# Routed experts in rounds of one, two or four, ranked by token count on the chip

## What is computed

```python
def moe_ffn(h, router_w, router_bias, w_gate, w_up, w_down, ws_gate, ws_up, ws_down):
    scores = sigmoid(xt @ router_w)                      # 256 tokens x 64 experts
    sel = scores + router_bias                           # 4 of 8 groups, then the top 8 experts
    wts = scores of the 8 chosen, / their sum * 2.5
    y = for each expert e:  (silu(x_e @ w_gate[e]) * (x_e @ w_up[e])) @ w_down[e],  times wts
    return sum over a token's 8 experts + the shared expert of the same form
```

## Time and profile before

| | us |
|---|---|
| median of 3 executions | 3715.33 |
| lowest, highest | 3712.76, 3722.76 |
| the profiled execution: its time, its span | 3722.76, 3722.7 |
| first layer's expert loop in it, first transposes to the first operation behind it | 342.95 to 937.40 |
| second layer's | 1251.00 to 1899.90 |
| busy: PE, PEld, DVE, ACT, POOL | 3370.9, 2469.4, 1214.7, 650.1, 215.4 |
| mean granted clock of PE | 0.956 |

### The profile page before, as it was taken

One profiled execution on the slowest core, in us unless ns is written; L12 is line 12 of the kernel. 1 busy time (PEld: TensorE's weight loads), 2 busy tenths in 40 slices (PEclk: granted clock), 3 DMA queues, 4 the chain that ended last, 5 costly groups with the idle time before them and its releaser, 6 DMA issues.

```text
span 3722.7 us, 68873 instructions
## 1 busy us (share of the span) xinstructions
PE 3370.9 (91%) x29944; PEld 2469.4 (66%) x29944; DVE 1214.7 (33%) x2371; ACT 650.1 (17%) x1258; POOL 215.4 (6%) x186
## 2 busy tenths in 40 slices
PE   7998899999888889999979999999998889887899
PEld 5776466666667556656657664448877777786788
DVE  1344132233334323323345452010324454444200
ACT  0111011111110111111123231000023313332100
POOL 0000000000000000000000000000004410341000
PEclk9998999999899899999989999999999999998999
DMA  7655398899474469969912351224431013100342
GB/s 275 221 216 224 152 386 331 349 402 385 161 273 154 181 245 372 402 274 382 392 67 81 137 191 68 79 78 149 147 141 48 4 34 125 37 4 3 128 155 102
DMA packets 116171, 703.07 MB, mean 189 GB/s; under 512 B 11296, under 2 KB 11472, under 8 KB 49760
## 3 DMA queue, kind: packets, MB, share of 16 engines
q1 hardware_dynamic: 112224, 685.47, 47.5%
q0 software_dynamic: 3584, 12.25, 1.0%
HBM read 696.62 MB, written 1.05 MB: 187 GB/s over the span
## 4 chain that ended last, share of the span: by engine, by line
PE 41%; DVE 5%; ACT 2%; issue 1%; POOL 1%; DVEq 0%; ACTq 0%; POOLq 0%; PEldq 0%
PE ps L1518 9%; PE ps L1505 9%; PE ps L2148 7%; PE ps L204 4%; PE ps L1855 4%; DVE arena L137 2%; ACT arena L120 1%; PE ps L544 1%; PE ps L571 1%; PE ps L342 1%; PE ps L2530 1%; PE ps L2160 1%; PE ps L2153 1%; DVE arena L141 1%; PE ps L559 1%
## 5 line engine op out<-in xcount | busy, mean ns | idle before, releaser
L204 PE MATMUL ps<-arena 128*128 128x256 f32 (+2 forms) x2432 | 637.8, 425 | 45.6 <-issue 17.1
L204 PEld LDWEIGHTS ps<-arena 128*128 128x128 f32 (+1 forms) x2432 | 475.8, 197 | 201.6 <-issue 124.6
L120 ACT ACTIVATE arena<-ps 128x512 f32<-128x512 f32 (+1 forms) x526 | 265.2, 504 | 1632.6 <-PE ps L204 384.9
L1098 PE MATMUL ps<-arena 128*64 128x256 f32 x4096 | 484.9, 387 | 33.1 <-issue 32.9
L1098 PEld LDWEIGHTS ps<-arena 128*64 128x64 f32 x4096 | 320.3, 140 | 198.1 <-issue 91.6
L2148 PE MATMUL ps<-arena 64*64 64x64 f32 x10496 | 310.4, 226 | 53.6 <-issue 19.5
L1505 PE MATMUL ps<-arena 128*128 128x512 f32 (+1 forms) x1024 | 334.1, 489 | 10.3 <-DVE arena L146 10.3
L2148 PEld LDWEIGHTS ps<-arena 64*64 64x64 f32 x10496 | 296.9, 141 | 67.7 <-issue 34.5
L1518 PE MATMUL ps<-arena 128*128 128x256 f32 x1536 | 332.0, 379 | 0.0
L1518 PEld LDWEIGHTS ps<-arena 128*128 128x128 f32 x1536 | 291.8, 190 | 40.1 <-issue 0.5
L137 DVE TENSOR_TENSOR arena<-arena,ps 128x512 f32<-128x512 f32 (+1 forms) x276 | 163.1, 591 | 461.1 <-PE ps L2148 237.9
(11 more groups left out here) (190 smaller groups left out, 2557.8 us busy)
## 6 DMA issues: line engine op xcount, KB each, us to landing
arena<-in_w_gate SPq DMA_DIRECT2D x128, 1024.0 KB, 8.5
arena<-in_w_up SPq DMA_DIRECT2D x128, 1024.0 KB, 11.7
arena<-in_w_down SPq DMA_DIRECT2D x128, 1024.0 KB, 8.9
arena<-in_mlp SPq DMA_DIRECT2D x80, 1024.0 KB, 4.7
arena<-in_w_ada SPq DMA_DIRECT2D x48, 1024.0 KB, 7.2
arena<-in_ada SPq DMA_DIRECT2D x48, 1024.0 KB, 4.8
arena<-in_w_in SPq DMA_DIRECT2D x30, 1024.0 KB, 5.6
arena<-in_w_rkv SPq DMA_DIRECT2D x20, 1024.0 KB, 4.8
```

The costliest lines, as they stand in the source:

```text
L120: self.e.activation(out, in_, func, bias=bias, scale=scale, **more).then_inc(*self.done(key))
L204: ins = pe.matmul(out, a, b, start=start and i == 0, stop=stop and i == len(pairs) - 1)
L1098: ins = pe.matmul(psum.of["gu", l, new][64 * ab:64 * ab + 64, i_ * 256:i_ * 256 + 256], xe[:, k, new % 2 * 128 + 64 * ab:new % 2 * 128 + 6 ...
```

## The change

The experts are no longer taken by number. Their counts of tokens are made on the chip, the experts are ranked by them, and the rank says in which *place* an expert is computed. The 64 places lie in 26 rounds (13 pairs) of one, two or four places, with 128, 64 or 32 slots each:

| pair | 0 | 1 | 2 | 3 | 4 | 5 | 6 | 7 to 11 | 12 |
|---|---|---|---|---|---|---|---|---|---|
| places in each of its two rounds | 2 | 1 | 4 | 2 | 4 | 1 | 4 | 2 | 4 |

Places 0 to 3 belong to experts 16 to 19 whatever their counts, so that their weights can be loaded before the ranking is known. The four fullest of the others go to the rounds of one, the next 24 to the other rounds of two, the last 32 to the rounds of four. Counts in the reference's inputs, from its own routing:

| layer | experts over 64, with their old rounds | in rounds of one | in rounds of two, most | in rounds of four, most |
|---|---|---|---|---|
| first | 109, 99, 73 tokens; rounds 2, 3, 14 | 109, 99, 73, 56 | 55 | 31 |
| second | 67, 75, 71, 73 tokens; rounds 1, 2, 19, 31 | 75, 73, 71, 67 | 63 | 30 |

What comes with it:

- **Before the loop, PE and DVE.** New matmuls count the tokens and turn the mask and the gates to expert-major (L1070 to L1079 of the changed kernel), five DVE operations rank the experts and make a permutation matrix, five more matmuls move mask, gates and numbers into rank order (L1113 to L1116), DVE copies them out, and only then come the matmuls of the places and all that hangs on them. The shared down projection is split in two halves around them.
- **SP.** From round 2 on every expert load first reads the expert's number from SBUF into a register, and its address in HBM is computed from it. Before the first of them SP waits for the numbers.
- **In the loop.** The same matmuls for each expert, on 128, 64 or 32 columns; all else once a round, so 26 times and not 32. The overflow test stands as it was, with 128, 64 or 32 as the limit.

```diff
+PLAN = (2, 1, 4, 2, 4, 1, 4, 2, 2, 2, 2, 2, 4)
+FIRST = (16, 17, 18, 19)
+WIDTH = [n for n in PLAN for _ in range(2)]
...
+        def expert_rows(sp, name, l, e):
+
+            if e < len(FIRST) or at.counting:
+                return D[name][l, FIRST[e % len(FIRST)]]
+            o = 192 + l * 64 + e
+            chosen = sp.value_load(flags[0:1, o:o + 1], min_val=0, max_val=63)
+            src = D[name][l, bass.ds(chosen, 1)]
+            return src.rearrange("o p j d -> (o p) j d" if name == "w_down" else "o p n -> (o p) n")
...
                 if new is not None:
+                    if new == 2:
+                        sp.wait_ge(*at["ids", l])
                     for name in ("w_gate", "w_up", "w_down"):
-                        for e in (2 * new, 2 * new + 1):
+                        for e in places_of(new):
+                            src = expert_rows(sp, name, l, e)
...
+                load(sp, (name, l, e), ("up", l, new), src, also=[("over", "pe", l, new)])
...
+            down(shared[2], True, False, (0,))
+            b, old = psum.hold(3, ("sorted", l), ("ids", l))
+            freed(pe, old)
+            reach(pe, *at["moved", l])
...
+            down(shared[2], True, False, (1,)).then_inc(*made(("shared", l)))
...
                 def hidden(i_, what):
-                    for ab in range(2):
-                        reach(pe, *at[what, l, 2 * new + ab])
+                    w = 128 // WIDTH[new]
+                    for e in places_of(new):
+                        reach(pe, *at[what, l, e])
                     for k in range(8):
-                        for ab in range(2):
+                        for ab in range(WIDTH[new]):
...
+            do.stt(E.at[:, 0:1], b[0:64, 64:65], 64.0, E.key_col[0:64, :], ALU.mult, ALU.add)
+            do.stt(E.keys, b[0:64, 0:64], 64.0, E.key_row[0:64, :], ALU.mult, ALU.add)
+            do.ts(E.keys, E.keys, E.at[:, 0:1], None, ALU.is_gt, None)
+            do.red(E.at[:, 1:2], E.keys, ALU.add)
+            do.ts(E.moved, E.rank_at[0:64, :], E.at[:, 1:2], None, ALU.is_equal, None, ("moved", l))
+            b = psum.of["sorted", l]
+            dve.wait_ge(*at["sorted", l])
+            do.cp(mk, b[:, 0:128], ("mask in order", l))
+            do.cp(flags[0:1, 192 + l * 64:256 + l * 64], b[0:1, 256:320])
```

More of the change, by code:

```diff
@@ L21, with places_of @@
 NPUMP = (2, 6)
+PLAN = (2, 1, 4, 2, 4, 1, 4, 2, 2, 2, 2, 2, 4)
+FIRST = (16, 17, 18, 19)
+WIDTH = [n for n in PLAN for _ in range(2)]
+NQ, NR = len(PLAN), len(WIDTH)
+BASE = [sum(WIDTH[:r]) for r in range(NR + 1)]
+assert BASE[-1] == 64 and 2 * PLAN[0] == len(FIRST)
+def places_of(r):
+    return range(BASE[r], BASE[r + 1])
 ARENA = 35144
@@ L1033, in moe_pe @@
                     .then_inc(*made(("shared gu", l, j)))
-            b, old = psum.hold(2, ("places", l), ("counts", l))
+            b, old = psum.hold(2, ("loads", l), ("moved", l))
             freed(pe, old)
-            reach(pe, *at["tri"])
-            reach(pe, *at["shared h", l, 1])
-            pe.matmul(b[:, 0:64], tri[:, 0:128], E.mk[:, 0:64], start=True, stop=True)
-            pe.matmul(b[:, 64:128], tri[:, 0:128], E.mk[:, 64:128], start=True, stop=False)
-            pe.matmul(b[:, 64:128], ones[:, :], E.mk[:, 0:64], start=False, stop=True)
-            pe.matmul(b[:, 128:192], ones[:, :], E.mk[:, 0:64], start=True, stop=False)
-            pe.matmul(b[:, 128:192], ones[:, :], E.mk[:, 64:128], start=False, stop=True).then_inc(*made(("places", l)))
+            reach(pe, *at["weighed", l])
+            for t in range(2):
+                pe.matmul(b[0:64, 0:64], ones[:, 0:64], E.mk[:, t * 64:t * 64 + 64], start=t == 0, stop=t == 1)
+            for t in range(2):
+                ins = pe.matmul(b[0:64, 64:65], E.mk[:, t * 64:t * 64 + 64], ones[:, 0:1], start=t == 0, stop=t == 1)
+            ins.then_inc(*made(("loads", l)))
+            b, old = psum.hold(3, ("by expert", l), ("by expert out", l))
+            freed(pe, old)
+            for i, (v, n) in enumerate(((E.mk, 64), (E.Gt, 65))):
+                for t in range(2):
+                    o = i * 256 + t * 128
+                    ins = pe.transpose(b[0:64, o:o + 128], v[:, t * n:t * n + 64], ident[:, :])
+            ins.then_inc(*made(("by expert", l)))
             for i in range(4):
@@ L1045, in moe_pe, with down @@
                 freed(pe, old)
-            def down(wd, first, last):
+            def down(wd, first, last, tiles_=(0, 1)):
                 wv = wd.rearrange("p (j d) -> p j d", j=2)
-                for t in range(2):
+                for t in tiles_:
                     for nh in range(2):
@@ L1068, in moe_pe @@
             reach(pe, *at["ws_down", l])
-            down(shared[2], True, False).then_inc(*made(("shared", l)))
+            reach(pe, *at["shared h", l, 1])
+            down(shared[2], True, False, (0,))
+            b, old = psum.hold(3, ("sorted", l), ("ids", l))
+            freed(pe, old)
+            reach(pe, *at["moved", l])
+            for t in range(2):
+                pe.matmul(b[:, t * 64:t * 64 + 64], E.mkT[:, t * 128:t * 128 + 128], E.moved, start=True, stop=True)
+            for t in range(2):
+                pe.matmul(b[:, 128 + t * 64:192 + t * 64], E.GtT[:, t * 128:t * 128 + 128], E.moved, start=True, stop=True)
+            pe.matmul(b[0:32, 256:320], E.index[0:64, :], E.moved, start=True, stop=True) \
+                .then_inc(*made(("sorted", l)))
+            down(shared[2], True, False, (1,)).then_inc(*made(("shared", l)))
+            b, old = psum.hold(2, ("places", l), ("counts", l))
+            freed(pe, old)
+            reach(pe, *at["tri"])
+            reach(pe, *at["mask in order", l])
+            pe.matmul(b[:, 0:64], tri[:, 0:128], E.mk[:, 0:64], start=True, stop=True)
+            pe.matmul(b[:, 64:128], tri[:, 0:128], E.mk[:, 64:128], start=True, stop=False)
+            pe.matmul(b[:, 64:128], ones[:, :], E.mk[:, 0:64], start=False, stop=True)
+            pe.matmul(b[:, 128:192], ones[:, :], E.mk[:, 0:64], start=True, stop=False)
+            pe.matmul(b[:, 128:192], ones[:, :], E.mk[:, 64:128], start=False, stop=True).then_inc(*made(("places", l)))
             for k in range(0, 8, 2):
@@ L1113, in moe_pe @@
                     reach(pe, *at["htt", l, p])
-                    for ab in range(2):
-                        reach(pe, *at["w_down", l, 2 * p + ab])
+                    w = 128 // WIDTH[p]
+                    for e in places_of(p):
+                        reach(pe, *at["w_down", l, e])
                     for nh in range(2):
```

105 lines of the change are left out of this document (64 added, 41 removed).

## The result

| | median, us | lowest to highest | ratio to before, 95% |
|---|---|---|---|
| before | 3719.05 | 3712.76 to 3724.66 | |
| the change | 3604.27 | 3600.54 to 3608.04 | 0.969 (0.9676 to 0.9703) |
| predicted | 3533 | 3490 to 3640 | |

The change is faster by 3.1%, 115 us where 182 were forecast. The profiled execution took 3605.11 us, its span is 3603.3.

The account below looks back on a forecast made before the run. PE and weight DMA nearly tie, with seven overflow blocks adding 203 us; without them transfer binds. Loops fall from 1243 to 1040 us (-203), ranking adds 21: -182, so 3533 us against the median, range 3490 to 3640.

Parts of the forecast that it names:

- A: Expert loops: overflow blocks vanish and the weights' transfer becomes the bound; own range 3490 to 3575 us, chance 0.55.
- B: Rounds of four: PE stays at the lower clock after its waits, 64 us in all, 3597 us; chance 0.2.
- C: Expert loads: tiles come slower through the register or from scattered experts; 3625 us at a tenth slower; chance 0.12.
- rival E: Expert loops: an overflow block still runs, one costs 29 us, giving 3565 us; chance 0.06.
- SP's 1.3 us for a tile: SP's queue: register load, DMA and address instruction cost 1.3 us a tile, hidden below the transfer's 2.51.
- D: SP's queue: each load costs more than 3.0 us, making the kernel slower; at 3.5 us 3850 us; chance 0.07.
- the forecast 10.6 each: Ahead of each layer's loop: counting, ranking and added DVE work cost 10.6 us a layer, 21 in all.
- the release 2.4 us later: Rounds of four: SP's next load was taken to start 2.4 us after the up projection ends.
- the term of 12 us for the eight rounds of four: Each layer's rounds of four: idle DMA time from slow projections after short waits, 12 us, bounds 0 and 44.
- the 30.5 us: Rounds of four: from one slot release to the next plus restart, 30.5 us against 32.3 when DMA engines run dry.
- the tile's price: Weights' transfer in the loops: one tile of 1.049 MB costs 2.51 us, at most 2.60.
- half of 18: Second layer's loop: three of six pump tiles fall in rounds of two; half their 18 us taken, 8 us counted.

Follow-up runs that it names:

- e3: The change with all 16 pairs as rounds of two, still ranked and loaded through registers (overflow blocks return): 3701.9 us.
- e2: The change without any overflow test in the rounds of four, their overflow handling left out on all three engines: 3560.8 us.
- g1: The change with the overflow block of a round of four handling only its last expert, the test kept: 3572.4 us.
- f1: The change with SP's wait for the w_gate and w_up slots moved from TensorE's overflow counter to ScalarE's: 3573.4 us.
- g2: f2 plus, in rounds of four but the last two, SyncE making the overflow test and freeing gate slots after the gate projection: 3553.4 us.
- f2: The change with DVE's rounding of x put ahead of its waits for the sorted and counted masks: 3591.3 us.
- e4: The change with 28 more transposes per expert in the never-run overflow block of the rounds of two: 3632.1 us.
- e1: The change with each round of four's overflow test split into two, each jumping over two experts' block: 3608.1 us.

## Why the prediction was off

The measured 3604 lies in the stated range, but 29 us above the own range of the forecast mechanism (A, to 3575). The room that it fell into was there for rivals B and C, which did not come true; that part is luck.

**Right in direction and in most of the mechanism.** No block ran: rival E falls. The loops became bound by the weights' transfer. PE waits 136.6 us in 15 stretches for in_w_gate, and in rounds of two the DMA engines are always busy. SP's 1.3 us for a tile was measured at 1.2 and is hidden (D falls), and tiles land 2.5 us apart through registers as without (C falls; e3). Rounds of four pack as forecast. 8.9 and 8.2 us ahead of the loops stand for the forecast 10.6 each, and PE's first gather comes 10.1 us later (344.92 for 334.78). That "the DMA engines are idle there" was read wrong: before, they are busy 0.72 of the time from 334 to 343 us. They fill the ring, in the change from 331 to 341, and are done ahead of the loop, so the added time counts all the same. The trace after has 415 GB/s over 123 us of rounds of two. The 358 GB/s of the Trainium skill, "DMA: Bandwidth & Descriptors", section "Where 436 GB/s comes from", by which about 3688 us would have come out, is not what holds here.

**The step that failed** is the sentence "the release 2.4 us later", in the term of 12 us for the eight rounds of four. It was measured on a round of two. In a round of four with its full block the release came 8.2 us after the up projection, since PE's branch stood for 6.0 us, over four experts' program text. With that, release to release is not the 30.5 us that "just fit" under 32.3 but about 36. The rows of a round's transposes between 410 and 560 us show it (first and last start, which are those of rounds 5 and 10): the change's, then e2's, g1's and f1's.

```profile
L1148 PEld LDWEIGHTS ps<-ident,arena x12: 140/142/230, 423.0 to 559.3; 128*128 128x128 f32 x12
```

```profile
L1148 PEld LDWEIGHTS ps<-ident,arena x12: 140/142/143, 421.9 to 543.5; 128*128 128x128 f32 x12
```

```profile
L1154 PEld LDWEIGHTS ps<-ident,arena x12: 140/142/143, 420.0 to 544.9; 128*128 128x128 f32 x12
```

```profile
L1148 PEld LDWEIGHTS ps<-ident,arena x12: 140/184/231, 424.4 to 555.7; 128*128 128x128 f32 x12
```

136.3 us, 121.6 without the test, 124.9 with the short block, 131.3 with the release by ScalarE. The step of a pair's second round of four alone, from its transposes to the next ones, takes 35.2 to 36.4 us in the change (six such steps), 28.5 to 31.3 in e2 and 29.4 to 31.4 in g1. The forecast 30.5 fits the short branch.

**The sizes of the rest.** Of the loops' 62 us over forecast (1102.4 for 1040), 33 go with the long branch (g1), 12 more with the test itself (e2), which I had counted at nothing in a round with slack. That was wrong, because the slack is PE's while the release is on the transfer's path. 17 are left: 1.5 from where the loop is taken to end, and the others, by an estimate that no run tested, the tile's price. Two windows of e2, one with rounds of four and one with rounds of two alone, have full DMA engines at 402 and at 414 GB/s:

```profile
490.00:580.00 90.00, 64.39 (x523) 43.67 (x522) 20.58 (x41) 11.55 (x20) 0.00 (x0) 0.89 0.98 402
...
660.00:803.00 143.00, 137.81 (x990) 95.58 (x989) 45.36 (x88) 27.11 (x47) 0.00 (x0) 1.00 1.02 414
```

A tile at 402 GB/s costs 2.61 us, the 2.6 that I had named as the most and left for 2.51; over half the tiles of a layer that is 9 us, 18 in both layers, by this estimate a little more than the 15.5 that are left.

The other terms can be set beside the DMA engines' idle time, added up from the packets over the stretches in which less than 0.6 of the engines' time is used. At the start it is 10 us a layer for the 11 forecast. At the rounds of one it is 17 and 24 us for 24. At and behind the rounds of four it is 29 and 30 us in the change and 11 and 13 in e2, for the 12 forecast: with the release at 2.4 us or less this term would have been right. Two slips of the sum change little: half of 18 is 9, not 8, for the pumps, and 3597 + 48 is 3645, not 3640, for the range's end.

**Rival B** gives 3597 and so lies nearest to 3604, but not by its mechanism. Its sign, idle DMA engines inside the rounds of four, did come, but the branch gives the same sign. After PE's wait of 12.49 us ahead of round 5's gate projection the clock is at its lower level (1.2 GHz, granted share 0.50), and that projection takes 5.9 us and not 3.66:

```profile
430.00:440.00 10.00, 4.03 (x40) 2.51 (x44) 0.00 (x0) 0.00 (x0) 0.00 (x0) 0.50 1.01 424
440.00:450.00 10.00, 8.64 (x127) 4.35 (x118) 1.50 (x2) 1.38 (x2) 0.00 (x0) 0.97 0.79 308
```

But by the up projection it is back at the full one (0.97, 2.4 GHz; 3.66 us), where B had all three projections at 7.1. What the 2.2 us at the gate projection cost was not tried by itself.

Of the 203 us forecast for the loops 142 were thus measured. Three quarters of the missing 61 (45) went into a wait that the change made itself, at the test of the rounds of four, where the text that a round skips is twice that of before; the rest is put down to the tile's price by an estimate. The fastest version, g2, gets 51 us back (3553.4), some 13 of them by f2's order of DVE's work, still with all overflow handling; with these inputs its overflow paths, as those of the change, are never taken, so only the path without overflow was timed.

## What to carry to other kernels

A branch over code that is never run is not free. On PE its price rose with the program text skipped, though not for every branch (e4), and it falls on everything that the same queue releases afterwards. Give buffers back ahead of such a test, or by an engine whose branch is short (ScalarE's took 45 ns here), and look at the queue's own branch rows, which no busy time shows. Where a transfer is the bound, a slack of 15 us on the computing engine hides its work but not a delay in what frees the next buffer: cost each such release by its own row, in the shape that the change will have.

## What was not expected of the hardware

PE's branch takes mostly 0.2 to 0.5 us (at most 2.4) over the text of one or two experts and 1.4 to 6.8 us over that of four. The long ones end 2.3 to 2.6 us after a 16 KB packet of program text starts, and this packet starts up to 4.4 us after the branch does. Splitting one jump in two does not help (e1); 28 more instructions an expert in the blocks of the rounds of two bring 9 of their 28 branches over 1 us, where 3 were before (e4). A load whose address comes from a register moved its megabyte as fast as any other, for 0.3 us of register load and 1.2 us of SP's queue in all.
